# A decay row spread by TensorE, a first weight piece in two halves, an earlier clearing and earlier freed expert slots in a two-layer diffusion step

## What is computed

```python
def _hyena_filter(L, f_w1, f_b1, f_w2, f_b2, f_w3, f_freq, decay):
    ...
    h = jnp.sin(f_freq * (feat @ f_w1 + f_b1))
    h = jnp.sin(f_freq * (h @ f_w2 + f_b2))
    h = (h @ f_w3).astype(jnp.float32) * jnp.exp(-t * jnp.abs(decay).astype(jnp.float32))
    return h[:, :D_MODEL], h[:, D_MODEL:]

def _hyena(x, w_in, ...):
    z = _short_conv(x @ w_in + b_in, conv_w, conv_b)
    x0, x1, v = jnp.split(z, 3, axis=-1)
    u = (v * x1).astype(jnp.float32)
    y = (_bidir_long_conv(u, h_fwd, h_bwd) + u * d_skip) * x0
    return y @ w_out + b_out

def _hier_moe(x, ...):
    # top group of 4, then the top 2 of its 4 experts; combine holds their weights
    for e in range(N_EXPERTS):
        a, b = jnp.split(t @ w_up[e], 2, axis=-1)
        y = y + combine[:, e:e + 1] * ((jax.nn.silu(a) * b) @ w_down[e])
```

## Time and profile before

| | |
|---|---|
| median of 3 runs | 1171.68 us (1169.81 to 1172.51) |
| the profiled execution's own time | 1167.03 us |
| its span, first to last instruction | 1164.8 us |
| busy share of the span | PE 89%, DVE 51%, ACT 17%, POOL 15% |
| read from HBM | 324.50 MB |
| chain that ended last | PE 66%, DMA 20%, DVE 7%, SP's queue 3% |

### The profile page before, as it was taken

The page is one execution under the profiler, slowest core; times in us unless marked ns, Lnnn a source line. Parts: engine busy times, 40 slices in busy tenths (PEclk is TensorE's granted clock), DMA queues, the critical chain, the costliest instruction groups (busy, mean ns, idle before and its releaser), DMA issues.

```text
span 1164.8 us, 25786 instructions
## 1 busy us (share of the span) xinstructions
PE 1035.4 (89%) x10508; PEld 617.8 (53%) x10508; DVE 596.9 (51%) x1385; ACT 196.9 (17%) x479; POOL 172.3 (15%) x211
## 2 busy tenths in 40 slices
PE   4899999999997999999759999999999999577992
PEld 1555555375553655666435554565455566344661
DVE  5338899645542333433269991475573343121345
ACT  4221111101310000010040010363231000000002
POOL 1200000320020111112101000154012111101110
PEclk9999999999998999999979999799989999998997
DMA  9964967940689999984999969333089999999912
GB/s 306 402 239 165 370 219 289 380 137 1 250 307 391 390 390 391 391 327 169 390 398 335 406 249 366 118 92 90 0 307 323 386 387 389 393 398 396 390 61 97
DMA packets 114787, 334.41 MB, mean 287 GB/s; under 512 B 11648, under 2 KB 24384, under 8 KB 114208
## 3 DMA queue, kind: packets, MB, share of 16 engines
q1 hardware_dynamic: 91696, 300.69, 68.5%
q0 software_dynamic: 6224, 23.03, 5.6%
q10 hardware_dynamic: 16800, 9.72, 3.0%
HBM read 324.50 MB, written 20.45 MB: 296 GB/s over the span
## 4 chain that ended last, share of the span: by engine, by line
PE 66%; DMA 20%; DVE 7%; SPq 3%; ACT 2%; issue 1%; POOL 1%; ACTq 0%; DVEq 0%
PE bank L668 63%; DMA ring<-in_moe_w_down 14%; DMA ring<-in_hy_w_in 3%; DMA ring<-in_na_w_qkv 2%; SPq L447 1%; POOL P L650 1%; PE bank L1066 1%; SPq L464 1%; ACT x L1204 1%; DVE P L1828 1%; DVE hT L1585 1%; SPq L531 1%; DMA row_beta<-in_ln_b 1%; DVE st L1771 1%; DVE ring L1408 1%
## 5 line engine op out<-in xcount | busy, mean ns | idle before, releaser
L668 PE MATMUL bank<-ring,xgT 128*32 128x256 f32 x4224 | 251.3, 390 | 31.2 <-DMA ring<-in_moe_w_up 30.6
L668 PE MATMUL bank<-hT,ring 128*128 128x384 f32 x640 | 213.9, 498 | 10.3 <-DMA ring<-in_hy_w_in 5.3
L668 PEld LDWEIGHTS bank<-ring,xgT 128*32 128x32 f32 x4224 | 146.1, 112 | 118.0 <-issue 27.5
L1736 DVE TENSOR_TENSOR he<-sa,bank 128x128 f32<-128x128 f32 x66 | 19.0, 288 | 349.5 <-ACT sa L1262 349.5
L668 PEld LDWEIGHTS bank<-hT,ring 128*128 128x128 f32 x640 | 124.3, 195 | 98.6 <-issue 12.1
L629 POOL TENSOR_TENSOR yg<-ysb,gate_s 128x256 f32<-128x256 f32 x128 | 90.7, 729 | 412.6 <-ACT ysb L1267 412.6
L1408 DVE CUSTOM_DVE_ANT_0 ring<-ring,ring 128x1024 f32<-128x1024 f32 x120 | 146.9, 1224 | 4.8 <-PE bank L668 1.0
L668 PE MATMUL bank<-ring,heT 128*32 128x256 f32 x2112 | 130.8, 389 | 17.1 <-DMA ring<-in_moe_w_down 17.1
L668 PE MATMUL bank<-yg,ohT 32*128 32x256 f32 x1632 | 107.3, 391 | 3.2 <-DVE yg L1765 3.2
L668 PEld LDWEIGHTS bank<-ring,heT 128*32 128x32 f32 x2112 | 65.2, 111 | 73.2 <-issue 41.8
L668 PEld LDWEIGHTS bank<-yg,ohT 32*128 32x128 f32 x1632 | 74.6, 184 | 36.3 <-issue 27.5
(11 more groups left out here) (235 smaller groups left out, 997.5 us busy)
## 6 DMA issues: line engine op xcount, KB each, us to landing
ring<-in_moe_w_up SPq DMA_DIRECT2D x64, 2048.0 KB, 25.6
ring<-in_moe_w_down SPq DMA_DIRECT2D x32, 2048.0 KB, 25.2
ring<-in_k_ada SPq DMA_DIRECT2D x15, 2048.0 KB, 16.5
ring<-in_w_ada SPq DMA_DIRECT2D x9, 2048.0 KB, 12.8
ring<-in_hy_w_in SPq DMA_DIRECT2D x6, 2048.0 KB, 15.1
ring<-in_na_w_qkv SPq DMA_DIRECT2D x6, 2048.0 KB, 19.1
slots<-in_k_zero POOLq DMA_DIRECT2D x2, 5632.0 KB, 30.1
group_row<-slots ACTq DMA_DIRECT2D x264, 32.0 KB, 5.1
```

Of the source, the lines that this page charges most:

```text
L668: return nc.tensor.matmul(out, lhsT, rhs, start=first, stop=last)
L1736: v.tensor_tensor(he[:], sa[:], ps[0][:, 128:256], ALU.mult).then_inc(S["he_ready"], 1)
```

## The change

It has four parts.

1. `dabs` is loaded as one row of 8 KB. DVE takes its absolute value in that row. PE multiplies a row of 128 ones (`ones`) with four stretches of 512 columns, which spreads the row over 128 partitions in PSUM, and DVE copies the four banks into `dabs`. The four products are groups of their own ("decay"), ahead of mlp1.
2. in_0 is loaded in two halves by rows, and its products run with k outermost, so that the four banks finish together. The load of `skip` waits for the decay groups.
3. GpSimd clears the row list after in_0 instead of in_1.
4. A load into the buffer of an up piece waits until the last up product of its expert, counted by `up_ready`, instead of the end of the expert. SP reads the number to wait for from NBi.

```diff
-            sp.dma_start(dabs[:], bass.AP(A["hy_decay"].tensor, A["hy_decay"].offset, [[0, 128], [1, 2 * D]])).then_inc(dabs_in, 16)
+            sp.dma_start(dabs[0:1, :], bass.AP(A["hy_decay"].tensor, A["hy_decay"].offset, [[0, 1], [1, 2 * D]])).then_inc(dabs_in, 16)
...
+            pe.wait_ge(row_ready, 1)
+            pe.wait_ge(ones_ready, 1)
+            for c in range(4):
+                mm(bank(G_AT["decay"] + c)[:, :], ones[:], dabs[0:1, 512 * c:512 * c + 512]).then_inc(group_ready, 1)
...
+            dve.wait_ge(dabs_in, 16)
+            row = dabs[0:1, :]
+            v.scalar_tensor_tensor(out=row, in0=row, scalar=-1.0, in1=row, op0=ALU.mult, op1=ALU.max).then_inc(row_ready, 1)
...
-                    dve.wait_ge(dabs_in, 16)
-                    v.scalar_tensor_tensor(out=dabs[:], in0=dabs[:], scalar=-1.0, in1=dabs[:], op0=ALU.mult, op1=ALU.max
-                                           ).then_inc(dabs_ready, 1)
+                    for c in range(4):
+                        g = G_AT["decay"] + c
+                        wait_group(dve, g)
+                        v.tensor_copy(dabs[:, 512 * c:512 * c + 512], ps[bank_of(g)][:, :]).then_inc(evacuated[g % 8], 1)
...
+                elif name == "in_0":
+                    i = W_AT[name]
+                    wait_slot_free(i)
+                    for b, landed in enumerate((in0_half, w_loaded[W_SLOT[i]])):
+                        sp.dma_start(w_view(i, 8, 512)[:, 4 * b:4 * b + 4, :],
+                                     A["hy_w_in"][0][512 * b:512 * b + 512, 0:512].rearrange("(k p) n -> p k n", p=128)).then_inc(landed, 16)
...
+                if s == 0:
+                    pe.wait_ge(in0_half, 16)
+                    for k in range(KT):
+                        if k == KT // 2:
+                            wait_weights(pe, i)
+                        for f in range(4):
+                            last = mm(bank(G_AT["in_0"] + f)[:, 0:TOK], w[:, k, f * 128:(f + 1) * 128], hT0[:, k, :], k == 0, k == KT - 1)
+                            if k == KT - 1:
+                                last.then_inc(group_ready, 1)
...
-            pool.wait_ge(group_ready, G_AT["in_1"] + 4)
+            pool.wait_ge(group_ready, G_AT["in_0"] + 4)
             clear_slots(0)
...
+                def wait_used(i):
+                    e, c = divmod(i, 3)
+                    if c == 2:
+                        sp.wait_ge(expert_done[l], e + 1)
+                    else:
+                        groups = sp.value_load(NBi[0:1, 17 + e:18 + e], min_val=1, max_val=MAX_BLOCKS)
+                        sp.wait_ge(S["up_ready"], groups)
...
                     elif i >= RING + EXTRA:
-                        sp.wait_ge(expert_done[l], (i - RING - EXTRA) // 3 + 1)
+                        wait_used(i - RING - EXTRA)
```

More of the change, by code:

```diff
@@ L87 @@
 _at = 0
-for _name, _n in [("mlp0", 1), ("mlp1", 1), ("filt0", 4), ("cond0", 2), ("filt1", 4), ("cond1", 2), ("filt2", 4), ("cond2", 4),
+for _name, _n in [("mlp0", 1), ("decay", 4), ("mlp1", 1), ("filt0", 4), ("cond0", 2), ("filt1", 4), ("cond1", 2), ("filt2", 4), ("cond2", 4),
                   ("xm0", 8),
@@ L770, in _ @@
                 i = W_AT[f"in_{s}"]
-                wait_weights(pe, i)
                 w = w_view(i, 8, 512)
-                for f in range(4):
+                if s == 0:
[7 more added lines that the diff above has]
+                                last.then_inc(group_ready, 1)
+                else:
+                    wait_weights(pe, i)
+                for f in range(4 if s > 0 else 0):
                     out = bank(G_AT[f"in_{s}"] + f)
```

13 lines of the change are left out of this document (10 added, 3 removed).

## The result

Four runs of each kernel, taken in turn on one chip, gave a median of 1157.12 us for the changed kernel (1156.11 to 1159.13) against 1170.74 us for the kernel before (1167.15 to 1172.51): a ratio of 0.9879, with a 95% interval of 0.9848 to 0.9910. That is 14 us less, 11 to 18 by the interval; the forecast was 9. Two single executions in later series, one of the kernel before at 2120.78 us and one of `wide_work` at 2129.35, took nearly twice the time and are left out of every figure.

What follows compares the result with a forecast made beforehand. The prediction took a chain of waits mostly on PE, passing to transfers at in_0 and in_3, as the bound. Gains 3.0 + 2.6 + 3.4 = 9.0 took 1167.03 to 1158.0, or 1162.7 on the median's scale; 8-in-10 range 1158.0 to 1168.0.

Steps and rivals of the forecast that it cites:

- The median of the runs is 4.65 above that execution, and on its scale the forecast is 1162.7: Last step, whole kernel: moves the forecast from the profiled execution's 1158.0 to the scale of the runs' median, 1162.7.
- Part 1, 3.0 forecast: At the start: hT0 ready at 42.0 lets in_0 start 3.2 earlier, counted as 3.0 for a possibly late row.
- I take two slow and two fast ones, 5.2: At the start on PE: the four spreading products, priced between 3.5 and 7, take 5.2 and end at 12.1.
- mlp1 [...] is done before 13.1: At the start on PE: mlp1, behind the four spreading products, ends before DVE's copies do at 13.1.
- half pace at the start: Rival, chance 0.20: all four spreading products run at half pace, in_0 starts only 1.0 earlier; sum 7.0, time 1164.7.
- F: Start of filt0 on PE: 18.78 before, forecast 17.5; hT0 was to be ready 24.45 after it.
- Part 2, 0 forecast: At in_0: splitting its load gives nothing beyond part 1, and the new product order's cost is hidden; 0.
- Part 3, 2.6 forecast: In the projection: earlier clearing leaves in_3 the queue nearly to itself, so PE's wait of 2.64 goes; 2.6.
- Everything after each part hangs on the chain in front of it, so the gains add: Summing step, whole kernel: the parts' gains add as 3.0 + 2.6 + 3.4 = 9.0.
- Part 4, 3.4 forecast: In layer 0's experts: up pieces issued 3.4 earlier at expert 10 bring the last down piece 3.4 sooner; 3.4.
- Where the queue is full all along (before 505, and in layer 1) an earlier issue brings nothing: 0: In the experts before 505 and in layer 1: part 4 gains 0, as the DMA queue is full.
- The rival that the clock stays up in in_0: Rival, chance 0.12: a shorter pause before in_0 keeps PE's clock up, giving back in_0's 1.8; time 1160.9.

Runs made afterwards that it cites:

- wide_work: Kernel before with part 1's row spreading, but the decay still loaded into 128 partitions and row 0 spread all the same; ratio 1.0019.
- p2_halves: Kernel before with part 2 only (in_0's load in halves, products with k outermost); ratio 0.9990.
- p23: Kernel before with parts 2 and 3 only (halves and earlier clearing); ratio 0.9932.
- no1: Changed kernel without part 1 (decay again loaded as 128 rows); median 1157.02 us, ratio 0.9913 against the kernel before.
- split1: Changed kernel, raw row spread by two products ahead of mlp1 and two behind, ACT taking the absolute value, second sine before first exponential; 1153.49 us, ratio 0.9888 against before.
- p3_clear: Kernel before with part 3 only (row list cleared one piece sooner); ratio 0.9967.
- after: The changed kernel with all four parts, as in the first comparison against the kernel before; median 1157.12 us, ratio 0.9879.
- p13: Kernel before with parts 1 and 3 only (row load with spreading, and earlier clearing); ratio 0.9956.
- p4_slots: Kernel before with part 4 only (up slots freed by the last up product); ratio 0.9987.
- after2: The full changed kernel measured a second time, with more runs, against the kernel before; median 1158.27 us, ratio 0.9934.
- after3: The full changed kernel measured a third time against the kernel before; median 1158.33 us, ratio 0.9928.

## Why the prediction was off

**The size.** Three comparisons gave ratios of 0.9879, 0.9934 and 0.9928, and the medians of the changed kernel are 1157.1, 1158.3 and 1158.3. The level of before moved more: single runs of it in the five later series, 129 of them, lie between 1158.31 and 1177.86, with a mean of 1166.9 and a standard deviation of 3.7. The 1171.68 on which the forecast's scale stood came from three runs, 4.8 above that mean. The sum of 9.0 is near the 7.7 and 8.4 of the larger comparisons. So the step that failed for the time is the last one, "The median of the runs is 4.65 above that execution, and on its scale the forecast is 1162.7": that offset belonged to three runs, and not to the kernel. From the mean of the 129, the same sum gives 1157.9. That the sum itself is near is luck in part: the terms of parts 1 and 4 were too high, that of part 3 was too low, and two places with a gain were put at nothing, as follows.

**Part 1, 3.0 forecast.** This term failed: in the three profiles of the changed kernel in_0 starts at 46.51, 46.03 and 46.02, against 45.17, 46.24 and 45.75 in the three of before, 0.5 later in the mean and not 3 earlier. The step that failed first is "I take two slow and two fast ones, 5.2": the four products took 7.19 in each profile. With it fell "mlp1 [...] is done before 13.1", which the sum's own numbers don't give either, since 1.65 of mlp1 behind 12.1 end at 13.8. mlp1 ended at 16.4, and DVE's second marg waited for it, until 16.45 (15.14 and 15.36 in the other two profiles), and not for the copies. The row's landing, 5.31 in the first profile against 4.5, was 4.00 and 4.22 in the others, so that price was right. The nearest rival, half pace at the start, put F at 19.7, and F is 21.05, 19.74 and 19.97; but it put in_0 at 44.2. From F to in_0 went 25.5 to 26.3, not 24.5: filt0 took 3.79 instead of 3.39 and the first conditioning products up to 3.13 instead of 1.92, and PE takes up in_0 some 0.35 after hT0 is done, which the sum had at nothing.

ACT's queue had a part that the sum had left out, a small one. The copies' end released ACT's first exponential, which stands ahead of the second sine: a table load, 2.00 of exponential and a second table load, to 20.26. The sine's argument was done at 20.10, so the sine lost under 0.2 by it. A one-row product was not cheaper than one of 128 rows: 0.90 for a record, against 0.47 at full pace, with its neighbours at half pace too (filt0 in 3.79, where filt1 takes 1.99). This agrees with the rule of the Trainium skill (TensorE: Matmul & The Clock Gate, section "Why this matters for your kernels") that the prediction quotes; no run has a one-row product at full pace. The Trainium skill (ScalarE: Activation LUTs, section "What ACT_TABLE_LOAD costs") gives 1283 ns for a table load and about as much again for a drain. The trace agrees on the first, 1.28, and shows no drain: the exponential ends at 18.96, the load starts at 18.98 and the sine at 20.28. What part 1 does bring is at in_3 and behind it, and only where part 3 is missing.

**Part 2, 0 forecast.** Right for the full change. Alone it is -1.2 with zero inside the interval, and the rows show a gain at the start: in the three kernels with the halves and without the row (p2_halves, p23, no1) in_0 starts at 44.15, 43.80 and 44.45, always released by hT0 and not by its load, against a mean of 45.3 without either. Part 1 takes this away again: with the row it starts between 45.17 and 46.51 (wide_work and split1 aside). Its order of products costs nothing, as forecast: from the first transform of the filter to the transposes of u, p23 takes 129.57 with it and p3_clear 129.57 without.

**Part 3, 2.6 forecast.** Right in place: the wait is gone. The size was the one of a single profile: from the first transform of the filter to the transposes of u, after, p3_clear and p23 are 2.9 shorter than the first profile of before, but 2.5 to 6.3 shorter than the seven kernels with the wait, 3.9 in the mean, as the clock can fall behind it. "Everything after each part hangs on the chain in front of it, so the gains add" was wrong for it and part 1, as p13 shows. The sum didn't suffer by that, since the gain that they share was counted once, under part 3.

**Part 4, 3.4 forecast.** The mechanism is right in layer 0: the piece is issued at 535.14, 3.4 earlier than expert 10's end would release it, and the last up piece is 2.7 nearer to it. The next issue comes at 536.10, behind a register load, 0.6 later than without it; that the run with the loads alone costs nothing shows them hidden there, and not here. The rest of the gain was lost on PE, which took up that piece after a pause of 3.78 and was granted 0.54 of the clock while it worked on it: 5.86 from there to the down products. In the kernel before it was 5.20 (586.95 less 581.75), at 0.72; its row and window:

```profile
581.75 3.44 PE L668 MATMUL bank<-ring,xgT 128*32 128x256 f32 x32 [3.35 <-DMA ring<-in_moe_w_up]
...
582.00:587.00 5.00, 4.74 (x60) 2.36 (x55) 1.39 (x5) 0.28 (x1) 0.00 (x0) 0.72 1.02 415
```

So 2.0 were left, and 2.3 in the mean of all profiles. "Where the queue is full all along (before 505, and in layer 1) an earlier issue brings nothing: 0" failed for layer 1: in five of the six kernels with part 4 its experts take 257.8 to 259.1, in the fourteen without it 260.0 to 262.4. The sixth, p4_slots, gained nothing there (262.4), and no run tells why.

**The clock.** The rival that the clock stays up in in_0 came true in the first profile (20.71 from in_0 to the filter's transform against 22.41, 67.58 less 45.17), but not in after2 and after3, where in_0 is no shorter; both lengths stand in kernels with and without each part. In the 129 runs of before, the mean granted clock of a run and its time go together, by -5.9 us for each 0.01. Its mean is 0.9539 in them and 0.9576 in the 16 runs of after2 and after3, an estimate of 2.2 us by that slope. The transposes of u and the inverse transform, 1.8 shorter in the three profiles of the changed kernel than in the three of before, are a place of it.

The account of the change, three profiles against three: the start -0.5, up to the transposes of u 3.9, these and the inverse transform 1.8, experts 10 to 15 of layer 0 2.0, the experts of layer 1 2.7, together 9.9 of the 10.4 by which the spans differ. The comparisons of many runs gave 7.7 and 8.4, and 9.9 lies within both intervals; the profiled executions of the changed kernel were all below its medians, by 0.6 to 3.2. What stays open is why the loads land 1 to 3 us sooner in every kernel with the spreading work (with the late clearing, in_3 in 20.2 to 21.4, in the seven without it 22.8 to 23.7). It is neither the megabyte spared nor the load of one row.

## What to carry to other kernels

Before you price an earlier start, write out every engine's queue between the moved operation and the point where the strands meet, and what stands behind an added product on the same engine: here the load was rightly freed, but four added products held up the network product behind them, and a version with two of them ahead of it and no absolute value in the strand (split1) gave 4.8 us. A wait can cost more than its length, as the granted clock can fall in the products behind it. Two edits that remove waits in one stretch may remove the same wait, and a pair run tells. Where runs of one kernel spread over 1%, a median of three or four is no base for a forecast or a verdict of this size: take the base, and the range, from the spread of many.

## What the runs showed of the hardware

- A standstill in the same group of products, on PE, DVE and ACT at once, with its release put down to something unseen ("remote", "issue"), in all kernels of some series and in none of others, the unchanged kernel among both. The gathering took 7.6 us without it and 9.4 to 10.1 or 12.7 to 12.9 with it. It came back by the end of expert 10 of layer 0, where a stretch of 288.4 to 289.2 ends in all twenty profiles.
- The wide load of the decay into 128 partitions was taken up at 11.3 to 12.1 us in ten profiles and at 9.7 in one (p3_clear), the one-row load at 4.0 to 4.5 in seven and at 5.3 in one, both issued at 1.65: 7 to 8 us for 1 MB in most, with one other small load behind it, where the engines later moved 397 GB/s.
- The same 2 MB load (the ada piece issued near 103), on a queue that had stood empty before it, took 7.5 to 7.9 us in kernels with the spreading work and 8.8 to 9.4 in those without. No run tells why.
- PE's first products took twice their later time (filt0 3.79 against filt1's 1.99) in windows whose granted clock reads 1.00. After the waits for in_0 and in_3 a slow stretch shows a granted clock of 0.50.
